# First weight sums of the feed-forward layers by an accumulating transfer, and eight more value units by seven products

## What is computed

```python
# first block, each of 2 layers
x = x + mixed @ w_out[i]
h = rms_norm(x, norm2_w[i])
g, u = jnp.split(h @ w_up[i], [D_FF], axis=-1)          # D_FF = 2816
g = depthwise_conv_centered(g, ffn_conv_w[i], ffn_conv_b[i])
x = x + (jax.nn.silu(g) * u) @ w_down[i]
# second block, each of 4 layers
shift1, scale1, gate1, shift2, scale2, gate2 = adaln(c, ada_w[i], ada_b[i])
y = mixer_i(x * (1.0 + scale1) + shift1)
x = layer_norm(DN_ALPHA * x + (1.0 + gate1) * y, ...)
h = x * (1.0 + scale2) + shift2
y = conv_ffn(h, ffn_w_up[i], ffn_conv_w[i], ffn_conv_b[i], ffn_w_down[i])
x = layer_norm(DN_ALPHA * x + (1.0 + gate2) * y, ...)
```

## Time and profile before

| | us |
|---|---|
| median of 3 runs | 2393.14 (2391.2 to 2394.5) |
| the profiled execution, device time | 2394.42 |
| its span in the trace | 2392.7 |
| TensorE busy | 2369.1 |
| VectorE busy | 1697.1 |
| ScalarE busy | 735.9 |
| GpSimd busy | 151.8 |

### The profile page before, as it was taken

The page is one execution under the profiler, slowest core; times in us unless marked ns, Lnnn a source line. Parts: engine busy times, 40 slices in busy tenths (PEclk is TensorE's granted clock), DMA queues, the critical chain, the costliest instruction groups (busy, mean ns, idle before and its releaser), DMA issues.

```text
span 2392.7 us, 43614 instructions
## 1 busy us (share of the span) xinstructions
PE 2369.1 (99%) x18252; PEld 2193.0 (92%) x18252; DVE 1697.1 (71%) x3169; ACT 735.9 (31%) x1498; POOL 151.8 (6%) x268
## 2 busy tenths in 40 slices
PE   9999999999999999999999999999999999999998
PEld 7878999987899998999998999997899999889998
DVE  6656887566599857798864599864477984638983
ACT  3441220144322121533032243123423331444421
POOL 2000000000020000000000021021000000000000
PEclk9999999999999999999999999999999999999999
DMA  7948776574887677577674487653334555335542
GB/s 217 246 134 261 245 258 216 152 186 119 246 273 238 223 252 219 177 255 251 235 245 123 155 273 252 205 188 115 114 123 150 169 168 168 106 118 165 167 161 97
DMA packets 403278, 458.49 MB, mean 192 GB/s; under 512 B 50751, under 2 KB 374776, under 8 KB 403084
## 3 DMA queue, kind: packets, MB, share of 16 engines
q1 hardware_dynamic: 370098, 340.53, 45.7%
q0 software_dynamic: 29936, 112.73, 13.6%
q10 hardware_dynamic: 3050, 2.46, 0.4%
HBM read 451.48 MB, written 1.29 MB: 189 GB/s over the span
## 4 chain that ended last, share of the span: by engine, by line
PE 93%; DVE 4%; DMA 1%; issue 1%; ACT 0%; ACTq 0%; DVEq 0%
PE job_bank L1138 36%; PE job_bank L1062 29%; PE job_bank L1117 10%; PE mix_bank L1117 4%; PE job_bank L1652 4%; PE job_bank L1146 1%; PE mix_bank L1571 1%; DMA sb_ring<-in_ffn_w_down 1%; PE mix_bank L1599 1%; PE job_bank L1627 1%; PE mix_bank L1613 1%; PE mix_bank L1093 0%; PE mix_bank L1943 0%; PE job_bank L1369 0%; PE mix_bank L1898 0%
## 5 line engine op out<-in xcount | busy, mean ns | idle before, releaser
L1062 PE MATMUL job_bank<-sb_h,sb_ring 128*128 128x256 f32 (+1 forms) x2336 | 522.1, 381 | 0.8 <-DVE sb_h L3418 0.8
L1062 PEld LDWEIGHTS job_bank<-sb_h,sb_ring 128*128 128x128 f32 (+1 forms) x2336 | 435.1, 189 | 69.0 <-issue 10.0
L1138 PE MATMUL job_bank<-sb_t,sb_ring 128*128 128x128 f32 x1808 | 239.5, 275 | 0.0
L3102 DVE SCALAR_TENSOR_TENSOR sb_arena<-sb_arena,sb_c_act 128x1024 f32<-128x1024 f32 x168 | 215.7, 1284 | 21.7 <-DMA sb_arena<-in_ada_w 16.6
L1138 PE MATMUL job_bank<-sb_h,sb_ring 128*128 128x128 f32 x1712 | 227.7, 276 | 2.0 <-ACT sb_kept L2180 2.0
L1138 PEld LDWEIGHTS job_bank<-sb_t,sb_ring 128*128 128x128 f32 x1808 | 220.4, 192 | 0.0
L1138 PEld LDWEIGHTS job_bank<-sb_h,sb_ring 128*128 128x128 f32 x1712 | 209.9, 192 | 8.1 <-issue 4.5
L3217 DVE SCALAR_TENSOR_TENSOR sb_arena<-sb_arena,sb_par 128x256 f32<-128x256 f32 x440 | 199.1, 494 | 15.0 <-ACT sb_arena L2225 11.1
L1138 PE MATMUL job_bank<-sb_t,sb_arena 128*128 128x128 f32 x1544 | 204.6, 275 | 0.6 <-DVE sb_arena L3157 0.6
L1138 PEld LDWEIGHTS job_bank<-sb_t,sb_arena 128*128 128x128 f32 x1544 | 188.1, 192 | 0.8 <-DVE sb_arena L3157 0.8
L1117 PE MATMUL job_bank<-sb_h,sb_ring 128*128 128x128 f32 x1600 | 184.1, 275 | 1.4 <-ACT sb_h L2538 1.4
(11 more groups left out here) (530 smaller groups left out, 3458.5 us busy)
## 6 DMA issues: line engine op xcount, KB each, us to landing
sb_arena<-in_ada_w POOLq DMA_DIRECT2D x96, 1024.0 KB, 7.2
sb_ring<-in_ffn_w_up SPq DMA_DIRECT2D x88, 1024.0 KB, 5.2
sb_ring<-in_w_up SPq DMA_DIRECT2D x44, 1024.0 KB, 6.4
sb_ring<-in_ffn_w_down SPq DMA_DIRECT2D x32, 1024.0 KB, 5.3
sb_ring<-in_w_in SPq DMA_DIRECT2D x24, 1024.0 KB, 6.2
sb_ring<-in_w_down SPq DMA_DIRECT2D x16, 1024.0 KB, 5.2
sb_ring<-in_hg_w_in SPq DMA_DIRECT2D x16, 1024.0 KB, 5.8
sb_ring<-in_ml_w_up SPq DMA_DIRECT2D x16, 1024.0 KB, 5.7
```

The lines of the kernel that those rows point to most:

```text
L1062: mm = pe.matmul(o, st, mv, start=(k0 + k == 0 and t == 0), stop=(k0 + k == kn - 1), skip_group_check=True)
L1138: mm = pe.matmul(o, st[:, k, :], mv[:, k, :], start=(first and k == 0), stop=(k == n - 1), skip_group_check=True)
L3102: ins = vec.scalar_tensor_tensor(out=o, in0=w, scalar=col, in1=o, op0=ALU.mult, op1=ALU.add)
```

## The change

- `FAST_VALUES` of the second block becomes values 1 to 9 in layer 0 and all of these but 5 in layer 1: eight more value units go by seven products.
- For every seven-product unit of the feed-forward layers (147 + 8 = 155), the first sum is no longer VectorE's L3152. GpSimd's queue issues an SBUF-to-SBUF DMA that adds a22 onto a21 (512-byte runs, four to a partition, 256 KB; three runs, 192 KB for the six-tile units), on two semaphores in turn. It waits for the unit's landing and for the sum two back. VectorE and TensorE wait for the transfer where they used L3152's result. The other nine units keep L3152.
- GpSimd's order in each layer: the early ada loads, the first sum, the wait for x, the second sum, three ada loads, and then an order that follows VectorE's: each sum ahead of the ada loads that become free at that point. The last four ada loads of a layer: two can go out before the down sums, two stand behind the last sum of the layer.

```diff
-FAST_VALUES = {1: ((1, 2, 3, 4, 5, 6, 7, 8, 9),) * L1, 2: ((1, 3, 5, 7, 9), (2, 4, 6, 8))}
+FAST_VALUES = {1: ((1, 2, 3, 4, 5, 6, 7, 8, 9),) * L1, 2: ((1, 2, 3, 4, 5, 6, 7, 8, 9), (1, 2, 3, 4, 6, 7, 8, 9))}
...
+        def first_sum(eng, unit):
+
+            if unit in added_no:
+                n = added_no[unit]
+                eng.wait_ge(added_in[n % 2], 16 * (n // 2 + 1))
+            else:
+                eng.wait_ge(s.form_first, first_no[unit] + 1)
...
+            def first_sums(stack, l):
+
+                for unit, _, kt in [made for job in fast_up(stack, l) + fast_down(stack, l) for made in job[1]]:
+                    n = added_no[unit]
+                    _, _, a21, a22 = corners(unit, kt)
+                    pool.wait_ge(unit_in[unit % RING], landed[unit])
+                    if n >= 2:
+                        pool.wait_ge(added_in[n % 2], 16 * (n // 2))
+                    pool.dma_start(a21, a22, accum_op=ALU.add).then_inc(added_in[n % 2], 16)
+                    yield
+
+            def ahead_of_vector(stack, l, sums):
+
+                layer = l if stack == 1 else l + 2
+                forms_done, ada_done = 0, ADA_UNITS * layer + ADA_EARLY[layer]
+                gates, values, _ = glu_jobs(stack, l)
+                ups = [job for both in zip(gates, values) for job in both]
+                made = [1]
+                for p in range(FT):
+                    made += [1 if p + 3 < FT and ups[p + 3][0] in fast_no else 0]
+                    made += [-1] * (ada_beside(layer, p + 1) - ada_beside(layer, p))
+                for count in made + [1, 1, 2] + [-1] * 2 + [2] + [-1] * (ADA_LATE - 2):
+                    if count >= 0:
+                        for _ in itertools.islice(sums, count):
+                            pass
+                        continue
+                    ada_done += 1
+                    n = next_load[0]
+                    if n < ADA_UNITS * L2 and n // ADA_UNITS == layer and ada_before[n] < ada_done:
+                        load_ada()
+                        yield
+
             for layer in range(L2):
+                stack, l = fast_stages[layer]
...
+                while next_load[0] < ADA_UNITS * layer + ADA_EARLY[layer]:
+                    load_ada()
+                sums = first_sums(stack, l)
+                next(sums)
+                pool.wait_ge(s.tail_x, 2 * layer + 1)
...
+                next(sums)
+                for _ in range(ADA_RING):
+                    load_ada()
+                for _ in ahead_of_vector(stack, l, sums):
+                    next(beside, None)
...
+            for _ in first_sums(2, L2 - 2):
+                pass
+            sums = first_sums(2, L2 - 1)
+            next(sums)
             pool.wait_ge(s.tail_x, 11)
...
-                pe.wait_ge(s.form_first, f + 1)
+                first_sum(pe, unit)
...
-                vec.tensor_tensor(a21, a21, a22, ALU.add).then_inc(s.form_first, 1)
-                own(s.form_first, form_no[unit] + 1)
+                if unit not in added_no:
+                    vec.tensor_tensor(a21, a21, a22, ALU.add).then_inc(s.form_first, 1)
+                first_sum(vec, unit)
                 form_free(vec, unit)
```

More of the change, by code:

```diff
@@ L457, in build @@
         ada_in = [sem(f"ada_in{i}") for i in range(ADA_RING)]
+        added_in = [sem(f"added_in{i}") for i in range(2)]
         bank_read = [sem(f"bank_read{i}") for i in range(4)]
@@ L714, in build @@
         form_no = {unit: n for n, unit in enumerate(fast_units)}
+        added_units = [unit for stack, l in fast_stages for job in fast_up(stack, l) + fast_down(stack, l)
+                       for unit, _, _ in job[1]]
+        added_no = {unit: n for n, unit in enumerate(added_units)}
+        first_no = {unit: n for n, unit in enumerate(unit for unit in fast_units if unit not in added_no)}
+        def first_sum(eng, unit):
[4 more added lines that the diff above has]
+                eng.wait_ge(s.form_first, first_no[unit] + 1)
         def form_slot(unit):
@@ L978, in tap_weights, with load_ada @@
                     yield
-            n = 0
+            next_load = [0]
+            def load_ada():
+                n = next_load[0]
+                layer, c = n // ADA_UNITS, n % ADA_UNITS
+                if layer == L2 - 1 and c == 6:
+                    pool.wait_ge(s.ho_read, 4)
+                if ada_before[n] is not None:
+                    pool.wait_ge(s.ada_acc, ada_before[n] + 1)
+                src = a["ada_w_2"][layer][c % 4 * 2 * P:(c % 4 + 1) * 2 * P,
+                                          c // 4 * ADA_COLS_AT_ONCE:(c // 4 + 1) * ADA_COLS_AT_ONCE]\
+                    .rearrange("(k p) c -> p k c", p=P)
+                pool.dma_start(ada_tile[n], src).then_inc(ada_in[ada_signal[n]], 16)
+                next_load[0] += 1
@@ L984, in _ @@
                     pool.wait_ge(s.unit_used, plan[("out1", layer)][0][1][0][0] + 1)
[L985 to L1004 removed]
+                while next_load[0] < ADA_UNITS * layer + ADA_EARLY[layer]:
[3 more added lines that the diff above has]
+                pool.wait_ge(s.tail_x, 2 * layer + 1)
+                if layer == L2 - 1:
+                    gate_loads()
+                if layer == L1 - 1:
+                    tap_loads()
+                beside = tap_weights() if layer == L1 - 1 else gate_weights() if layer == L2 - 1 else iter(())
+                next(sums)
[3 more added lines that the diff above has]
+                    next(beside, None)
+                for _ in itertools.chain(beside, sums):
+                    pass
+                assert next_load[0] == ADA_UNITS * (layer + 1)
             pool.wait_ge(s.tail_x, 8)
@@ L1029, in _ @@
                 pool.dma_start(dst, row.to_broadcast([P, D])).then_inc(s.fin_in, 16)
+            for _ in sums:
+                pass
         @block.tensor
```

18 lines of the change are left out of this document (removed).

## The result

The changed kernel takes 2474.9 us (median of 4 runs, 2471.0 to 2481.5) against 2392.8 before (4 runs, 2391.2 to 2394.5): **1.034 times, interval 1.033 to 1.036, slower**. Forecast were 2390.9 with 2384 to 2404. The profiled execution is the slowest of the four, 2481.5 us with a span of 2479.8.

What follows compares the result with a forecast made beforehand. TensorE was taken to bound the kernel (busy 2369.1 of 2392.7 us), VectorE nearly a second bound in the second block's layers 0 and 1. Profiled 2394.4 - 5.3 - 3.6 + 1.0 + 5.7 = 2392.2, median 2390.9 us, range 2384 to 2404.

Steps and rivals of the forecast that it cites:

- The sum as a transfer: All transferred sums: time S from the unit's landing to the sum's signal, 4.2 us, bounded by 2.9 and 6.5.
- In the ups this is covered: Ups: VectorE takes units mostly 4 to 12 us after landing, forms 2 to 10 us ahead of TensorE's third quarter.
- Not covered at the last unit of d2: Last d2 unit of all six layers: TensorE waits for the sum, +5.7 us, despite quicker loads in four layers.
- GpSimd's order: GpSimd's queue: later ada loads and a third sum behind ada loads cost nothing at the centre, up to 2 us a layer.
- -3.6 at 713 us: First block, layer 1: TensorE's 1.82 us wait and the half-clock stretch behind it go as VectorE is relieved, -3.6 us.
- -5.3 for the values: Eight more value units by seven products save TensorE 0.66 us each, 5.3 us, if forms come in time.
- +1.0 for VectorE's pace: Ups of the second block's layers 0 and 1: VectorE at 95 and 97%, 0.5 us of new TensorE waits each.
- Quick sums: Rival: sums take about 3 us, last-unit waits shrink to +1.6, VectorE's to 0: 2385.8 us; chance 0.32.
- By the engines: Rival: ups of four layers with ada loads, 3.2 us of all DMA engines a sum, about 2430 us; chance 0.07.
- the share near 1 that the prediction named as a sign: Sign of a wrong prediction: a DMA engine share near 1 in the middle of the ups.
- S alone: Rival: at 6.5 us from landing to signal, last d2 units cost 17.3 us: 2402.5 us; chance 0.19.
- It doesn't do what it says: Rival: the 713 us wait has another cause, so -3.6 stays out: 2394.6 us, within the 0.42 main case.

Runs made afterwards that it cites:

- e3_late_sums: Kernel before, with first sums by transfer only in the second block's layers 2 and 3, ada-load loop as before: 2424.0 us, 1.0134.
- quarter sums: Changed kernel with each transferred sum cut to the first of its three or four runs a partition: 2405.8 us, 1.0057 times the kernel before.
- e13_two_values: Kernel before with GpSimd's tap products later and one more seven-product value unit in each of the second block's layers 0 and 1: 2387.4 us, 0.9974.
- e2_sums: Changed kernel with the old list of value units, all first sums by transfer: 2483.9 us, 1.0376 times the kernel before.
- e5_order: Kernel before with the changed GpSimd queue order and its waits for landings, no transfers, VectorE making all first sums, old values: 2406.6 us, 1.0055.
- e4_late_traffic: Kernel before plus transfers onto unawaited scratch in the second block's layers 2 and 3, VectorE keeping its sums: 2393.5 us, 1.0001.

## Why the prediction was wrong

Of the 82 us, 13.5 are GpSimd's order and about 77 (2483.9 less 2406.6) the sums' slowness; the values bring back about 9.

- **"The sum as a transfer", S = 4.2 us: right where nothing else is under way, and that was the wrong number to take.** Alone it is 4.4 us from landing to signal. But 121 of the 155 take longer than 4.5 us from issue to landing, all but three of them with a ring or ada load under way, and the medians are 6.5 to 8.1, at and above the 6.5 that I gave as the upper end. The engines spend 2.1 us on a sum (0.324 x 140 / 22), less than the 3.2 that I allowed, so it is not the work but the company that made it long. The small load that I called like the sum goes in 16 packets of 4 KB, the sum in some 500 of 512 bytes; as a lower end its 2.6 us did hold. A rate in company has to be taken from company.
- **"In the ups this is covered": the step that failed.** It compares forms with TensorE's third quarter. In layers 2 and 3 that comparison holds: TensorE waits for no form and no sum in their ups. What it leaves out is that VectorE waits in its order, so that what the sum delays is not its own forms but the joins and taps behind them. The prediction asked of a wait "what is queued behind it" for GpSimd and not for VectorE. In the four layers with ada loads the comparison itself fails: 23.1 of TensorE's 30.3 us of waits in the ups are for sums and forms. There the room of 4 to 12 us behind a landing was put against S = 4.2, while the sums took medians of 7.1 to 8.4 in these ups and up to 24.2 behind ada loads. All this cost 54.2 us over the six layers, 4.8 of them the order's.
- **"Not covered at the last unit of d2", +5.7: the mechanism was right, the size was not, and it is not only the last unit.** The downs lost 30.7 us, of which the order alone is 6.9 by the table. At the six last units it is 9.5 (1.3, 1.4, 3.0, 1.4, 1.4, 0.9 in the order of the layers). The first unit of d2 costs about as much again, 9.3, and the rest lies ahead of it; I had put nothing there. The last unit's load got quicker as I said, even more (4.3 us for the 768 KB in the second block's layer 0, 8.6 in the earlier trace rows). But the ada loads that made room for it now go out right behind the sum, and it takes 7.6 us. DMA issues at 1203 to 1222 us and GpSimd's queue there, after:

```profile
sb_ring<-in_ffn_w_down SPq DMA_DIRECT2D x1, 768.0 KB, 4.3
...
sb_ring<-sb_ring POOLq DMA_DIRECT2D x1, 192.0 KB, 7.6
```

```profile
1220.74 1.27 POOL L1018 DMA_DIRECT2D sb_ring<-sb_ring  x1 [12.34 <-DMA sb_ring<-in_ffn_w_down]
1221.49 1.98 POOL L1007 DMA_DIRECT2D sb_arena<-in_ada_w  x2
```

  From landing to signal it was 5.2 to 7.9 us at the six last units. In `e3_late_sums` the first unit of layer 2's d2 lost 4.9 us (3.3 at its second and third quarter, 1.6 in slower records behind them), the second nothing, the last one 5.1.
- **"GpSimd's order", nothing, up to 2 us a layer: mis-sized.** 13.5 us. I counted the two ada loads at the end of a layer and the third sum at its start; VectorE's waits for ada units rose all along the ups, to 70 us, without any sum.
- **-3.6 at 713 us: wrong cause.** I took VectorE's load; it was GpSimd's tap product blocking a VectorE product, and moving this product later gave 3.3 us of the layer (174.6 to 171.3). In the changed kernel the wait is 3.7 us instead of 1.8.
- **-5.3 for the values: the price was right**, 2.6 us in layer 0 with the quarter sums and 0.65 a value in `e13_two_values`. The +1.0 for VectorE's pace wasn't seen in layer 0; in layer 1 it was 2.3 us of waits for forms, more than the 0.5 given. Without the relief the eight values cost 10.3.
- **The rivals.** *Quick sums* is what the quarter kernel does, less the order. *By the engines* gave the nearest time, 2430, and its 1.8 us of engine time a sum was passed (2.1). In layers 2 and 3 it is refuted: at a share of 0.88 TensorE lost nothing. Whether the traffic costs in the four layers with ada loads is open. For it: the share near 1 that the prediction named as a sign stands there, and the ring loads of these ups took medians of 7.2 to 8.2 us instead of 5.4 to 7.5. Against it: TensorE waits for no ring load, and in `e2_sums` against `e5_order` the sums cost these layers 5 to 11 us each, the two without ada loads 16 and 19. But that last point is weak, since in the changed kernel they cost 10 to 14 us against 12 and 13. *S alone* had the right mechanism at the units it counted, and too few units. *It doesn't do what it says* had its condition met: the wait at 713 us has another cause.

## What to carry to other kernels

When an in-order engine is to wait for something slower than its own work, look not only at the consumer of that result but at everything queued behind the wait; the time in hand is that of the tightest operation behind it; here the cost set in between medians of 4.5 and 5.3 us. Price a transfer from rows in which the other queues are busy, not from the quiet corner of the trace, and look at every unit of a chain, not only at the tightest. And test the two halves of such a trade each alone: the values that the relief made room for were worth 5 to 9 us, the slow sums cost 77 and the order of the queue 13.5.

## What the runs showed of the hardware

- A 256 KB adding transfer inside SBUF, in runs of 512 bytes, takes 4.2 us from issue to landing alone, 3.1 for 128 KB, 2.3 for 64 KB; a plain copy of 256 KB 2.7. The Trainium skill, DMA: Bandwidth & Descriptors, Anatomy of one DMA, gives an estimated 3.2 us for 256 KB with twice the reading; the measurement is 1.0 above it. Collectives: The Full Stack, The bandwidth ceiling, has an adding step of a collective run at half the rate of a copying one; inside SBUF an adding transfer takes 2.6 times a copy's engine time here.
- GpSimd's instruction for an adding transfer of 256 KB takes 1.31 us, for 64 KB 0.88, against 0.74 for a plain copy of 256 KB.
- DMA engines at a share of 0.88 beside a TensorE without a gap (`e4_late_traffic`, 1830 to 1970 us): a share that high alone cost nothing there. At 1.06 (kernel after, 1080 to 1142 us) TensorE was busy 57.58 of 62 us; whether the share has a part in that is open.
- From landing to signal an adding transfer of 256 KB took 4.4 us with nothing else under way and 6.5 to 8.1 in the medians of the six layers; right behind three 1 MB loads of the same queue it took 17.9 from issue to landing.
- A GpSimd product of 1.98 us stretched a VectorE product from 0.69 to 2.59 us (kernel before, 712 us).
